# Adding the experts' rows into x on the chip with one-hot matrix products, in place of a scatter to memory and a read back

## The reference, cut to what matters

```
    def expert_block(args):
        xblk, e = args
        return (jax.nn.silu(xblk @ w1[e]) * (xblk @ w3[e])) @ w2[e]
...
    out = jnp.zeros_like(hf).at[row_tok].add(yb * row_w[:, None].astype(yb.dtype))
...
        x = x + hier_moe(h, w_group[l], b_group[l], w_expert[l], b_expert[l], w1[l], w3[l], w2[l])
    return rms_norm(x, g_final)
```

## Time and profile before

| | before |
|---|---|
| median of 3 runs | 1858.24 us (1854.73 to 1860.97) |
| the profiled execution: its time, its span | 1859.26 us, 1857.5 us |
| PE busy | 1701.7 us, 92% of the span |
| DVE, ACT, POOL busy | 712.4, 594.9, 169.2 us |
| read from HBM, written | 329.75 MB, 18.87 MB |
| mean granted TensorE clock | 0.978 of full |
| chain that ended last | PE 70%, DMA 19%, DVE 5%, ACT 4% |

### The profile page before, as it was taken

One profiled execution on the slowest core, in us unless ns is written; L12 is line 12 of the kernel. 1 busy time (PEld: TensorE's weight loads), 2 busy tenths in 40 slices (PEclk: granted clock), 3 DMA queues, 4 the chain that ended last, 5 costly groups with the idle time before them and its releaser, 6 DMA issues.

```text
span 1857.5 us, 24733 instructions
## 1 busy us (share of the span) xinstructions
PE 1701.7 (92%) x10405; PEld 1297.4 (70%) x10405; DVE 712.4 (38%) x1529; ACT 594.9 (32%) x1048; POOL 169.2 (9%) x128
## 2 busy tenths in 40 slices
PE   7999999997998877778889999997999899999998
PEld 5878766886564444444468966766788798888886
DVE  4355345454111111211135567555734532222223
ACT  3434354422011000000134456554624432222222
POOL 1000110221111111101001000011101000000221
PEclk9999899998999999999999999998999999999999
DMA  7512100358899999999994331012420232223201
GB/s 259 182 46 91 47 23 23 122 195 339 350 411 408 410 395 407 404 409 407 427 361 180 94 110 66 1 46 108 176 91 12 91 103 91 91 87 137 93 23 46
DMA packets 79580, 341.90 MB, mean 184 GB/s; under 512 B 8007, under 2 KB 15815, under 8 KB 66024
## 3 DMA queue, kind: packets, MB, share of 16 engines
q1 hardware_dynamic: 73192, 329.76, 46.0%
q0 software_dynamic: 5120, 8.40, 1.4%
q10 hardware_dynamic: 1152, 2.10, 0.3%
HBM read 329.75 MB, written 18.87 MB: 188 GB/s over the span
## 4 chain that ended last, share of the span: by engine, by line
PE 70%; DMA 19%; DVE 5%; ACT 4%; issue 2%; SPq 0%; POOL 0%; DVEq 0%; POOLq 0%; ACTq 0%
PE ps L553 66%; DMA arenaf<-in_w 14%; DMA arenaf<-in_mem 3%; DMA hf<-in_w_xkv 2%; PE ps L972 1%; PE ps L2881 1%; DMA ring<-in_w_in 1%; ACT splitr L629 1%; DVE arenaf L2963 1%; PE ps L807 1%; DVE splitr L618 0%; DVE arenaf L2981 0%; ACT arenaf L961 0%; PE ps L2059 0%; DVE xf L3259 0%
## 5 line engine op out<-in xcount | busy, mean ns | idle before, releaser
L553 PE MATMUL ps<-hr,splitr 128*128 128x512 f32 (+1 forms) x2784 | 579.1, 367 | 6.9 <-POOL hr L904 4.3
L553 PEld LDWEIGHTS ps<-hr,splitr 128*128 128x128 f32 x2784 | 476.5, 193 | 88.9 <-issue 5.1
L553 PE MATMUL ps<-splitr,hr 128*128 128x512 f32 (+1 forms) x1488 | 273.7, 343 | 2.2 <-DVE hr L1069 1.4
L553 PEld LDWEIGHTS ps<-splitr,hr 128*128 128x128 f32 x1488 | 234.2, 189 | 35.8 <-issue 2.0
L618 DVE TENSOR_TENSOR splitr<-ring,splitr 128x2048 fp32r<-128x2048 f32 x61 | 142.9, 2343 | 232.8 <-ACT splitr L629 232.6
L629 ACT CAST splitr<-ring 128x2048 fp32r<-128x2048 f32 x61 | 116.1, 1905 | 152.0 <-PE ps L553 142.7
L2096 DVE SCALAR_TENSOR_TENSOR tq<-ps,arenaf,tq 128x256 f32<-128x256 f32 x32 | 15.5, 484 | 268.8 <-PE ps L553 236.3
L2132 ACT COPY junk<-ps 64x512 f32<-64x512 f32 x32 | 18.5, 578 | 288.8 <-PE ps L553 288.8
L553 PE MATMUL ps<-arenaf,tq 128*64 128x512 f32 x336 | 81.5, 629 | 31.0 <-DMA arenaf<-in_w 31.0
L553 PE MATMUL ps<-arenaf 128*64 128x128 f32 (+7 forms) x784 | 103.0, 342 | 5.5 <-ACT arenaf L979 3.5
L618 DVE TENSOR_TENSOR splitr<-arenaf,splitr 128x2048 fp32r<-128x2048 f32 x27 | 62.2, 2303 | 104.9 <-ACT splitr L629 104.9
(11 more groups left out here) (395 smaller groups left out, 1926.0 us busy)
## 6 DMA issues: line engine op xcount, KB each, us to landing
ring<-in_w SPq DMA_DIRECT2D x22, 2048.0 KB, 43.1
arenaf<-in_w SPq DMA_DIRECT2D x22, 2048.0 KB
splitf<-in_w SPq DMA_DIRECT2D x21, 2048.0 KB, 44.0
hf<-in_w SPq DMA_DIRECT2D x20, 2048.0 KB, 44.5
ring<-in_w_in SPq DMA_DIRECT2D x11, 2048.0 KB, 9.6
otf<-in_w SPq DMA_DIRECT2D x11, 2048.0 KB
ring<-in_w_gate_up SPq DMA_DIRECT2D x7, 2048.0 KB, 7.9
arenaf<-in_w_in SPq DMA_DIRECT2D x4, 2048.0 KB
```

The source lines that it names most:

```text
L553: return te.matmul(out, lhsT, rhs, start=start, stop=stop)
```

## The change

The weighting and the adding move from the end of the stage into the blocks. Nothing is scattered and nothing is read back.

- **Router.** One index list instead of two. A further group of 32 products (`ps7`, "slot weights") works out for each slot the token's number as a float (`idf`) and the weight (`wsc`), both on all 128 partitions; DVE forms their operand OW8 once the weights exist, and copies both out.
- **Result of a block.** ACT writes the weighted result, rounded to the fp32r format, to 64 partitions of `Y2W` (the high part, two instructions of 64x512); DVE writes the remainder, with its sign turned as the instruction gives it, to the other 64 partitions (two instructions of 64x512). DVE also builds `SEL`, 128 slots by 512 tokens, one where the slot's token is that token.
- **Sum.** For b - 2 PE multiplies SEL by Y2W: 4 token tiles by 2 halves, 8 products of 512 columns, 4 behind each of the two parts of `pe_up`, into four PSUM banks kept for them; DVE adds each of the 8 banks to x. All else in the stage shares the other four banks.
- **Last blocks.** The sums of blocks 30 and 31 are accumulated together behind `pe_down(31)` (`pe_last_sums`, 16 products), and 8 additions follow.
- **Combine.** The read back and `rows_added` go; the norms wait for the last additions. The final gain is loaded by ACT's queue at block 31. The gain of the memory tokens moves from block 30 to 29, and one step of the extra blocks' places to the head of block 24.

```
+                ps = take("slot weights")
+                for w, values in enumerate((B8.bitcast(F32), OW8)):
+                    for n in range(8):
+                        for m in range(2):
+                            it = mm(ps[CAP * m:CAP * m + CAP, 32 * w:32 * w + 32], R8[:, n, :], values[:, n, :],
+                                    n == 0, n == 7)
...
+                vstep(ve.tensor_tensor(OW8, O8, W8.broadcast_to([128, 8, 32]), ALU.mult), ("slot weights",))
...
+                vstep(ve.tensor_scalar(idf, bank("slot weights")[:, 0:32], 1024.0, None, ALU.add))
+                vstep(ve.tensor_copy(wsc, bank("slot weights")[:, 32:64]), ("wsc",), ("free", "slot weights"))
...
-            def ge_scatter(b, sig):
-                ge.indirect_dma_start(out=yd, out_offset=bass.IndirectOffsetOnAxis(ap=places(b, 1), axis=0),
-                                      in_=YO[b % 2][0:CAP, :], in_offset=None, bounds_check=1023,
...
             def se_down(b):
-                se.copy(YO[b % 2][0:CAP, 0:512], bank("down", b)[0:CAP, :]).then_inc(
-                    *se_done("scalar copies", ("y", b, 0), ("free", "down", b)))
+                for half in range(2):
+                    ps = slice(CAP * half, CAP * half + CAP)
+                    se.activation(Y2W[b // 31][half][ps, :], bank("down", b)[ps, :], ACT.Copy,
+                                  scale=wsc[ps, b:b + 1]).then_inc(*se_done("weighted rows high", ("yhi", b, half)))
...
             def ve_down(b):
-                ve.tensor_copy(YO[b % 2][0:CAP, 512:1024], bank("down", b)[CAP:2 * CAP, :]).then_inc(
+                ve.tensor_scalar(SEL[b // 31], IOTA, idf[:, b:b + 1], None, ALU.is_equal).then_inc(
+                    *ve_done("slots of tokens", ("sel", b)))
+                for half in range(2):
...
+                    for w in ve_at(("down", b), ("yhi", b, half), ("wsc",)):
+                        ve.wait_ge(*w)
+                    ve.scalar_tensor_tensor(y[other, :], bank("down", b)[ps, :], wsc[ps, b:b + 1], y[ps, :].bitcast(F32),
+                                            ALU.mult, ALU.subtract).then_inc(
...
+            def row_sum(ps, b, half, t, start, stop):
+                return mm(ps[:, :], SEL[b // 31][:, 128 * t:128 * t + 128], Y2W[b // 31][half], start, stop)
...
+            def pe_sums(b, half):
+                for t in range(4):
+                    ps = take("xc", b, half, t, banks=SUMS)
+                    row_sum(ps, b, half, t, True, True).then_inc(*pe_done("token sums", ("xc", b, half, t)))
...
+            def pe_last_sums():
+                order = [(half, t) for t in range(4) for half in range(2)]
...
+                for half, t in order[:4]:
+                    row_sum(take("xc", 31, half, t, banks=SUMS), 30, half, t, True, False)
+                for i, (half, t) in enumerate(order):
+                    for w in pe_at(("sel", 31), ("yhi", 31, half), ("ylo", 31, half)):
+                        te.wait_ge(*w)
+                    if i >= 4:
+                        row_sum(take("xc", 31, half, t, banks=OTHERS), 30, half, t, True, False)
+                    row_sum(bank("xc", 31, half, t), 31, half, t, False, True).then_inc(
...
+            def ve_sum(b, half, t):
+                ve.tensor_tensor(xs, xs, bank("xc", b, half, t)[:, :], ALU.add).then_inc(
...
                     if b < 32:
-                        pe_up(b)
+                        pe_up(b, 0)
+                        if b > 1:
+                            pe_sums(b - 2, 0)
+                        pe_up(b, 1)
+                        if b > 1:
+                            pe_sums(b - 2, 1)
...
             def sp_combine():
-                for t in range(4):
-                    sp.dma_start(G2[t], yd[256 * t:256 * t + 256, :].rearrange("(p k) n -> p (k n)", k=2)).then_inc(
...
                 def root(t):
-                    for w in se_at(("combined", t)):
+                    for w in se_at(("xsum", 31, 0, t), ("xsum", 31, 1, t)):
```

More of the change, by code:

```diff
@@ L132, in build @@
         OT, OTr = both("ot", 4096)
-        junk = sb("junk", 2048)
+        junk, junk_r = both("junk", 2048)
         con = sb("con", NCON)
@@ L1720, in ve_wo @@
                     ve.wait_ge(*w)
-                for w in range(2):
-                    ve.tensor_scalar(vals_r[w], vals[w], 7168.0, None, ALU.add)
+                ve.tensor_scalar(tokens, val1, 7168.0, None, ALU.add)
+                for t in range(4):
+                    ve.tensor_scalar(IOTA[:, 128 * t:128 * t + 128], iota, 128.0 * t, None, ALU.add)
                 ve.memset(Cn[:, 4, :].bitcast(F32), 0.0)
@@ L1803, in pe_router @@
                 it.then_inc(*pe_done("ranks", ("root sum",)))
+                ps = take("slot weights")
+                for w in pe_at(("slot weights",)):
+                    te.wait_ge(*w)
[4 more added lines that the diff above has]
+                                    n == 0, n == 7)
+                it.then_inc(*pe_done("ranks", ("weight sum",)))
             def se_store_rows(half, t):
@@ L2029, in x_se_down @@
                     se.wait_ge(*w)
-                se.copy(YO[b % 2][0:CAP, 0:512], bank("down", b, 0)[0:CAP, :]).then_inc(
+                se.activation(YX[:, 0:512], bank("down", b, 0)[0:CAP, :], ACT.Copy,
+                              scale=sx[0:CAP, NXC + b - 32:NXC + b - 31]).then_inc(
                     *se_done(f"{sig}scalar copies", ("y", b, 0), ("free", "down", b, 0)))
@@ new lines, in ve_down @@
+                for half in range(2):
+                    ps = slice(CAP * half, CAP * half + CAP)
+                    other = slice(CAP - CAP * half, 2 * CAP - CAP * half)
+                    y = Y2W[b // 31][half]
+                    for w in ve_at(("down", b), ("yhi", b, half), ("wsc",)):
+                        ve.wait_ge(*w)
+                    ve.scalar_tensor_tensor(y[other, :], bank("down", b)[ps, :], wsc[ps, b:b + 1], y[ps, :].bitcast(F32),
+                                            ALU.mult, ALU.subtract).then_inc(
+                        *ve_done("weighted rows low", ("ylo", b, half), *([("free", "down", b)] if half else [])))
@@ L2143, in pe_experts @@
+            def ve_sum(b, half, t):
+                xs = X3[:, t, 512 * half:512 * half + 512]
+                for w in ve_at(("xc", b, half, t), *STORED):
+                    ve.wait_ge(*w)
+                ve.tensor_tensor(xs, xs, bank("xc", b, half, t)[:, :], ALU.add).then_inc(
+                    *ve_done("x summed", ("xsum", b, half, t), ("free", "xc", b, half, t)))
             def pe_experts():
+                pool[0] = OTHERS
                 pe_rows(0)
@@ L2172, in pe_memory @@
                     for half in range(2):
-                        ps = take("norm", "mem", t, half)
+                        ps = take("norm", "mem", t, half, banks=SUMS)
                         for w in pe_at(("normed", "mem", t)):
@@ L2213, in ve_experts @@
                 for b in range(33):
+                    if b == 24:
+                        go(places_, 1)
+                    if 2 <= b < 32:
+                        for t in range(4):
+                            ve_sum(b - 2, 0, t)
                     if b < 32:
                         ve_hidden(b)
+                    if 2 <= b < 32:
+                        for t in range(4):
+                            ve_sum(b - 2, 1, t)
                     if b < 31 and b % 2:
@@ L2223, in ve_experts @@
                         ve_memory_scale()
-                    elif b == 30:
+                    elif b == 29:
                         ve_memory_gain()
+                for t in range(4):
+                    ve_sum(31, 0, t)
+                    ve_sum(31, 1, t)
                 S.close("ve", "experts")
@@ L2320, in extra @@
                 with eng.If(n > 0):
-                    for w in at(*S.ends("experts"), *ROWS_OUT):
+                    for w in at(*S.ends("experts")):
                         eng.wait_ge(*w)
@@ L2390, in sp_combine @@
             def sp_combine():
-                for w in sp_at(*S.ends("experts"), *ROWS_OUT):
+                for w in sp_at(*S.ends("experts")):
                     sp.wait_ge(*w)
-                for t in range(4):
-                    sp.dma_start(G2[t], yd[256 * t:256 * t + 256, :].rearrange("(p k) n -> p (k n)", k=2)).then_inc(
-                        *sp_done(f"expert rows back {t}", ("ldy", t), by=16))
-                    if t == 1:
-                        sp.dma_start(gfin, io["g_final"].partition_broadcast(128)).then_inc(
-                            *sp_done("final gain", ("gfin",), by=16))
                 sp.dma_start(wgt, io["w_gt"]).then_inc(*sp_done("gate weights", ("wgt",), by=16))
```

158 lines of the change are left out of this document (85 added, 73 removed).

## The result

| | before | after |
|---|---|---|
| median | 1858.35 us (20 runs, 1852.66 to 1861.68) | 1862.87 us (20 runs, 1858.62 to 1867.62) |
| ratio | | 1.0024, 95% interval 1.0015 to 1.0034 |
| profiled execution's span | 1857.5 us | 1861.3 us |
| first key on PE (start in the span) | 953.54 us | 953.58 us |
| from the first key to the end of the span | 904.0 us | 907.7 us |

The change makes the kernel 4.5 us slower, where 1.7 us faster was forecast (1856.5 us). The last two rows hold the surprise. In this pair of profiles the stage that was changed ends where it ended; the loss lies behind it, in code that the change does not touch. Profiles are therefore compared stretch by stretch.)

What follows compares the result with a forecast made beforehand. Weight loads were taken to bound the expert blocks, PE nearly the last three. Router +1.05, scatters -11.0, blocks 28 to 31 +3.0, stage end +5.3: -1.7 us, 1856.5 us; 8-in-10 range 1849 to 1864.5 us.

Steps and rivals of the forecast that it cites:

- Everything behind it moves with it.: Code behind the first key on PE shifts with that key's start, forecast from 953.54 to 951.8 us, -1.7 us.
- Router, +1.05 us: At the router, 32 added products start pe_up(0) 2.07 us late; its first half then ends 1.05 us later.
- Scatters, -11.0 us: Up to the memory tokens, 27 scatters removed at 0.41 us of all 16 DMA engines each save 11.0 us.
- PE stays inside its slack: In the expert blocks, PE with eight sums needs 14.2 us a block against the loads' 15.9 us.
- Blocks 28 to 31, 47.5 us from restart to `pe_down(31)`: Last blocks: 44.5 us, less 3.1 of waits, plus 6.1 for 24 sums and ACT; +3.0 us.
- End of the stage: From pe_down(31) to the first key: hand-overs 2.25 us, twelve sums 3.0 us, then the branch; +5.3 us.
- kept stall of 3.73 us: Before the first key: the branch's cost from the end of PE's last product stays 3.73 us.
- The wait before tile 2's transposes,: Behind the keys, at 986 us: PE's first x-dependent wait remains, so removing the read back shortens nothing there.
- The branch was waiting for the keys' load: Rival, 22%: before the first key, an earlier load makes the branch cost almost nothing; key at 948.3, kernel 1850.8 us.
- The sums cost more: Rival, 14%: in the expert blocks weight loading is not hidden, a sum costs 0.44 us; kernel 1864.2 us, slower than before.
- The scatter was a load on the engines: Opposite of a 6% rival: scatters were no DMA load in the expert blocks, 11.0 us go missing, kernel 1867.5 us.
- The bank additions: Rival, 5%: DVE's additions hold up PE's next sums, some 1 us a block behind block 28; 1860 us, no measurable change.

Runs made afterwards that it cites:

- after_same: The changed kernel run again unchanged, as base of its group: 1863.8 us, ratio 1.0028 to the kernel before.
- after_banks: The changed kernel with the ring of eight PSUM banks set on by five behind the experts, at position 5 as before: 1853.8 us, ratio 0.9975.
- after_banks6: The changed kernel with its ring of PSUM banks set on by 6 behind the experts: 1853.6 us, ratio 0.9972 to the kernel before.
- after_banks7: The changed kernel with its ring of PSUM banks set on by 7 behind the experts: 1856.8 us, ratio 0.9991 to the kernel before.
- after_banks1: The changed kernel with its ring of PSUM banks set on by 1 behind the experts: 1865.7 us, ratio 1.0035 to the kernel before.
- after_banks_late: The changed kernel with its ring set on by 5 only behind the third mixer of the second block: 1858.4 us, ratio 0.9998 to the kernel before.
- before_banks: The kernel before with its ring of PSUM banks set on by three behind the experts, at position 0: 1865.6 us, ratio 1.0037.
- banks_slots: after_banks with the 32 slot-weight products moved behind block 0's first pe_up half and DVE's two copies behind its first row gain: 1854.7 us, ratio 0.9991.
- before_scatter16: The kernel before with scatters of blocks 0 to 26 cut from 64 rows to 16, read back partly from another array: 1852.5 us, ratio 0.9967.
- after_nobranch: The changed kernel without the extra blocks' code and the compare and branch past it, on every engine: 1859.0 us, ratio 1.0004 to the kernel before.
- banks_short_sums: after_banks with the sum products of blocks 2 to 29 cut from 512 columns to 64: 1854.1 us, ratio 0.9976 to the kernel before.
- banks_memory: after_banks with the memory tokens' work one block later on ACT, DVE and PE: 1853.2 us, ratio 0.9975 to the kernel before.

## Why the prediction was wrong, point by point

- **What failed: "Everything behind it moves with it."** The stage's end was forecast 1.7 us earlier; in the one pair of profiles it is 0.04 us later, and over the seven profiles of the changed stage with its branch and with no other edit in the stage (after, after_same, after_banks, 6, 7, 1, late) it is 1.1 us shorter than before's 497.4. This part was right within a us, with some luck (below: +1.8 and -1.3 us that nearly cancel). But the code behind did not move with it. `pool[0] = OTHERS` and `pool[0] = RING` stand in the diff, and that the ring comes back at another position was not worked out. before_banks shows its price with nothing else changed: 6.4 us.
- **Router, +1.05 us:** `pe_up(0)` starts 2.25 us late against the slot roots (forecast 2.07), but in banks_slots nothing of it shows at the squares: 0 to 1 us by the spread of the profiles.
- **Scatters, -11.0 us:** that they cost, and about this much, before_scatter16 shows; the 0.41 us itself is not confirmed. It shared the queue's 26.0 us equally between gathers and scatters, but after the change the gathers alone have 0.8% of 1861.3 us, 14.9 us, which leaves 0.35 us for a scatter. Router and scatters together were -9.95; the changed stage's squares start 429.5 us behind the slot roots (mean of eight, after_nobranch included) and before's 439.3 (mean of two): -9.8.
- **"PE stays inside its slack":** right in its result (banks_short_sums), not in its picture. From 480 to 750 us PE, with 14.6 us a block (14.2 forecast), never waits: it works off matrices that were loaded ahead, and its first waits for loads come only behind 750 us, 2.9 us in all up to 880. The forecast period of 15.9 us near 700 us does not show.
- **Blocks 28 to 31, 47.5 us from restart to `pe_down(31)`:** 49.3 in the profile after. 24 sums at 0.28 instead of 0.25 us are 0.7 us, and the first `pe_up` behind the idle time, 5.68 us instead of 4.65, is 1.0 us.
- **End of the stage:** from `pe_down(31)` to the first key 11.3 us, forecast 12.6. The kept stall of 3.73 us is 2.35: the packet comes sooner, with emptier DMA engines. I also left the clock as it was. Here it stays up (0.55 became 1.00), some 3 us of gain that the sum does not have. A shorter stall does not secure this: in after_banks the stall is 2.06 us and the clock in the first 2 us of the keys 0.50 (first row; second row: the kernel after).

```profile
948.86:950.86 2.00, 2.00 (x5) 1.64 (x6) 0.00 (x0) 1.98 (x2) 0.00 (x0) 0.50 0.23 60
953.58:955.58 2.00, 2.00 (x9) 1.78 (x10) 0.27 (x1) 2.00 (x2) 0.00 (x0) 1.00 0.28 72
```

- **The wait before tile 2's transposes,** the first product behind the keys: it stays, 1.65 us for 1.71.
- **Rivals.** "The branch was waiting for the keys' load" is half right: it waits for the loads' traffic, not for that load, and so never costs "almost nothing": 1.85 us of idle PE at the least, in after_banks1. The measured 1862.9 us lies near the 1864.2 us of "The sums cost more", but by coincidence: the sums at 0.28 us decide nothing, as against 0.44 (and the bound above which they would, by the prediction's own terms (15.9 - 12.21) / 8, is 0.46 and not 0.45). The scatter was a load on the engines. The bank additions never hold PE up, but a bank far behind the stage does; no case had that.
- **How the two effects add up.** The clock at the keys blurs it: in the first 2 us behind the first key it is 1.00 in after, after_banks7, after_banks1 and after_banks_late (stalls of 1.85 to 2.35 us), 0.50 in after_banks and after_banks6 (2.06 and 2.25 us), 0.69 in after_same. So I count to and from the first product behind the keys. From the slot roots to it, before and before_banks take 537.3 and 537.2 us, the seven changed ones 533.6 to 534.7: the stage with the keys brings 3.2 us. From it to the end the kernels at position 0 take 870.1 to 870.8 us (after, after_same, after_nobranch, before_banks), those at position 5 862.4 to 864.2 (before included): the position costs 5.9 to 8.4 us. The 5.4 us of the medians at position 5 and the 1.8 us at position 0 lie on either side of 3.2 us, within their intervals.
- **What stays open.** At position 5 that last stretch has two values, 862.4 (after_banks, banks_memory) and 863.9 to 864.2 us (the other four); a part of it is for how long the clock stays low near 1250 us, which no run isolates. Nor does a run show why the clock at the keys fell behind a stall of 2.06 us and not behind one of 2.35. before_scatter16 has, besides, a second halt of 1.93 us among its keys, put down to issue; none of the others idles for more than 0.7 us there.

The version that beats both is after_banks (or after_banks6): 1853.8 us, 5.4 us or 0.25% below the kernel before.

## What to carry to other kernels

Whatever is handed out in turn (PSUM banks, buffers, semaphores) carries a counter out of a changed stage into all later ones. Compare it at the stage's end, before and after, and if it differs, look in the list of takes for one that gets a bank whose reader is still at work. A position can then be chosen; one wait was forecast from the list as 5.6 us and came as 5.66.
A taken branch behind a stage that fills the DMA engines can hold up the engine that is in a hurry: here it idles for 1.85 to 4.42 us. The branch also swallows gains made just ahead of it (banks_memory, banks_short_sums).
A releaser named by the profile is the event that came last. Where a branch (953.34) and an addition (953.23) end within 0.11 us of each other, ahead of a key at 953.58, only taking one away tells which it was.
When an experiment leaves out a part of some work, read from the page how much is really gone: three quarters of the entries were half of the bytes, and an eighth of the columns was half of the time.

## What the runs showed of the hardware that was not expected

- PE's branch ended 1.39 to 1.45 us behind the end of a 16,384-byte instruction packet in all thirteen kernels that have the branch. The packet started 3.9 us behind the branch's start at a DMA share of about 1, and 1.0 us behind it at 0.53.
- A PE wait of 5.66 us was followed by 24 products in 8.46 us, where 5.7 us is usual: the granted clock was at 1.2 GHz for a part of them. With 2.73 us it was 4.46 us for twelve instead of 2.97.
- A group of four sums of 128x512 took 1.12 us, 0.28 us a sum, while inside the long row of last sums they start 0.23 us apart (948.04 to 948.27 in after_nobranch with the key as the next). With 64 columns a group took 0.56 us, 0.14 us a sum. What the group's further 0.2 us are spent on is not shown.
